# Hybrid decoder layer on one core: the second token tile's x/B/C, z and v behind the first tile's output projection, query weights by head, and an interleaved start of the expert gathers

## What is computed

```python
proj = x @ w_in                                  # 256 tokens x 1024
q, k, v, iq, ik, iw, z, xbc, dt = split(proj)
attn = dsa_attention(q, k, v, iq, ik, iw)        # 8 heads x 64, the 64 best causal keys per query by an indexer
ssd  = ssd_mixer(z, xbc, dt, ...)                # conv over 4 tokens, silu, scan in two chunks of 128, gated RMS norm
h    = layer_norm(alpha * x + concat(attn, ssd) @ w_out)
q2   = h @ wq                                    # PEER: 8 heads x 2 x 128
s1, s2 = q2[:, :, 0] @ k1.T, q2[:, :, 1] @ k2.T  # 128 keys a side
eidx, gate = best 16 of the 16 x 16 sums         # per token and head
out  = layer_norm(alpha * h + sum_k gelu(h . u[eidx_k]) * gate_k * v[eidx_k])
```

## Time and profile before

| | us |
|---|---|
| median of 3 runs | 832.15 (830.57 to 832.9) |
| the profiled execution | 831.91 |
| its span | 830.2 |
| busy in it: PE, DVE, ACT, POOL | 556.6, 555.6, 438.6, 275.5 |
| share of the chain that ended last: waits for gathered rows | 42% |

### The profile page before, as it was taken

The page is one execution under the profiler, slowest core; times in us unless marked ns, Lnnn a source line. Parts: engine busy times, 40 slices in busy tenths (PEclk is TensorE's granted clock), DMA queues, the critical chain, the costliest instruction groups (busy, mean ns, idle before and its releaser), DMA issues.

```text
span 830.2 us, 10063 instructions
## 1 busy us (share of the span) xinstructions
PE 556.6 (67%) x3215; PEld 465.0 (56%) x3215; DVE 555.6 (67%) x1387; ACT 438.6 (53%) x768; POOL 275.5 (33%) x267
## 2 busy tenths in 40 slices
PE   6999999999978546374745445525556555454596
PEld 3478565788978536364645444524455554454542
DVE  3499674675767585858495858469858576767454
ACT  1123560218657747565565657537756566565532
POOL 0000000125346444343525253514654435434400
PEclk9999999999999886776777686767776777767789
DMA  8994402198999999999999999999999999999992
GB/s 300 391 352 148 158 1 68 60 400 327 423 421 421 421 420 422 422 420 422 423 421 422 420 421 421 422 419 380 422 421 421 422 422 423 420 422 422 421 422 120
DMA packets 54276, 301.01 MB, mean 363 GB/s; under 512 B 5432, under 2 KB 7776, under 8 KB 21472
## 3 DMA queue, kind: packets, MB, share of 16 engines
q0 software_dynamic: 36864, 268.45, 78.2%
q1 hardware_dynamic: 16160, 31.92, 10.6%
q10 hardware_dynamic: 1216, 0.19, 0.1%
HBM read 299.49 MB, written 1.05 MB: 362 GB/s over the span
## 4 chain that ended last, share of the span: by engine, by line
DMA 43%; PE 32%; DVE 12%; issue 6%; ACT 4%; POOL 2%; DVEq 0%; SPq 0%; POOLq 0%; ACTq 0%
DMA arena<-in_expert_uv,expert 42%; PE bank L634 7%; PE bank L434 7%; PE bank L616 5%; DVE arena L1341 4%; PE bank L654 3%; PE bank L475 3%; PE bank L570 3%; POOL arena L401 2%; ACT arena L918 2%; ACT weight L908 1%; DMA arena<-in_w_idx 1%; PE bank L425 1%; PE bank L541 1%; PE bank L624 1%
## 5 line engine op out<-in xcount | busy, mean ns | idle before, releaser
L634 PE MATMUL bank<-ident,arena 128*128 128x128 f32 x1920 | 307.9, 334 | 248.6 <-ACT arena L918 248.4
L401 POOL DMA_INDIRECT arena<-in_expert_uv,expert x256 | 273.8, 1070 | 512.1 <-PE bank L634 271.1
L634 PEld LDWEIGHTS bank<-ident,arena 128*128 128x128 f32 x1920 | 288.5, 177 | 267.3 <-ACT arena L918 267.0
L1341 DVE SCALAR_TENSOR_TENSOR arena<-x_sb,arena 128x1024 f32<-128x1024 f32 x256 | 306.7, 1223 | 169.8 <-DMA arena<-in_expert_uv,expert 169.6
L918 ACT ACTIVATE arena<-arena,weight 128x1024 f32<-128x1024 f32 x240 | 256.2, 1138 | 1.9
L903 ACT ACTIVATE gelu<-dots 128x4 f32<-128x4 f32 (+2 forms) x68 | 13.9, 204 | 206.5 <-DVE arena L1341 205.9
L434 PE MATMUL bank<-arena,x_t 128*128 128x512 f32 (+1 forms) x160 | 66.6, 574 | 8.1 <-DMA arena<-in_w_idx 8.1
L616 PE MATMUL bank<-x_t,arena 128*128 128x128 f32 x512 | 58.8, 275 | 1.3 <-ACTq L878 1.3
L616 PEld LDWEIGHTS bank<-x_t,arena 128*128 128x128 f32 x512 | 57.9, 192 | 1.5 <-ACTq L878 1.5
L908 ACT ACTIVATE weight<-gelu,gate 128x1 f32<-128x1 f32 x256 | 55.1, 284 | 3.2
L434 PEld LDWEIGHTS bank<-arena,x_t 128*128 128x128 f32 x160 | 31.0, 197 | 40.1 <-issue 37.4
(11 more groups left out here) (195 smaller groups left out, 444.4 us busy)
## 6 DMA issues: line engine op xcount, KB each, us to landing
arena<-in_w_in SPq DMA_DIRECT2D x6, 2048.0 KB, 14.5
arena<-in_peer_wq SPq DMA_DIRECT2D x4, 2048.0 KB, 7.9
arena<-in_w_out SPq DMA_DIRECT2D x2, 2048.0 KB, 21.9
arena<-in_expert_uv,expert POOLq DMA_INDIRECT x256, 25.9
arena<-in_w_idx SPq DMA_DIRECT2D x2, 608.0 KB, 8.1
x_t<-in_x_columns SPq DMA_DIRECT2D x2, 512.0 KB, 6.6
x_sb<-in_x SPq DMA_DIRECT2D x1, 1024.0 KB, 17.3
ln_gb<-in_ln_g SPq DMA_DIRECT2D x2, 512.0 KB, 10.2
```

The lines of the kernel that those rows point to most:

```text
L401: pool.indirect_dma_start(out=arena[:, slot * SLOT:(slot + 1) * SLOT], out_offset=None, in_=expert_uv, in_offset=bass.IndirectOffsetOnAxis ...
L634: last = mm(banks[2 * tile + k // 4][:, (k % 4) * P:(k % 4 + 1) * P], lhsT=arena[:, at + k * P:at + (k + 1) * P], rhs=ident[:, :], is_tran ...
L1341: ins = stt(rows, x_rows[:, bass.ds(tile * D_MODEL, D_MODEL)], 1.0, rows, ALU.mult, ALU.mult, accum_out=dots[:, parity, j:j + 1])
```

## The change

- The first stage is split by tile. x/B/C, z and v of tile 1 (`project_xbc(1, n)`, `proj_z`, `proj_v`), its cb, y_off, y_diag and attention come behind tile 0's output product, layer norm, first queries and first scores. x/B/C is made as (tile, half of the channels), 32 products of 128 columns each; the last tap of the convolution and its bias move from DVE to ACT (`take_xbc`).
- Query weights come by head (`load_head`, 1 MB each) instead of by two heads. Head 0 lies in `mix`, heads 1 and 2 in slots 10 and 11, heads 3 to 7 one after the other in `mix`, each load behind tile 1's queries of the head before. Scores are made per head, those of heads 4 to 7 within units 2 to 4.
- The first gathers go into slots 12 to 15, 4 and 5 (`first_slots`), each used up to three times in units 0 and 1. Units 0 and 1 work in groups of two slots, interleaved by hand with the rest of tile 1 on PE, ACT and DVE. The units from 2 to 8 are unrolled; before, units 3 to 6 were a loop.
- q's weights are loaded into the buffers of x and of the norm's rows, the input and index weights in four parts instead of two. All copies of probabilities are on ACT.

```diff
-    jobs += [("proj_k", 0)] + idx_dots[0] + [("proj_k", 1)] + idx_dots[1]
-    jobs += [("T_qk", 0, 0), ("T_qk", 0, 1), ("proj_xbc", 0), ("consts",), ("proj_xbc", 1)]
...
+    jobs = [("proj_idx", t) for t in both] + [("proj_q", t) for t in both] + [("T_idx", t) for t in both] + [("consts",)]
+    jobs += [("proj_k", 0)] + idx_dots[0] + [("proj_k", 1)] + idx_dots[1] + sums[0]
+    jobs += [("T_qk", 0, 0), ("T_qk", 1, 0), ("proj_xbc", 0, 0)] + logits[0] + [("T_qk", 0, 1), ("T_qk", 1, 1), ("proj_xbc", 0, 1)]
...
+    jobs += [("proj_xbc", 1, 0), ("T_h", 0, 0), ("T_h", 0, 1), ("peer_q", 0, 0), ("key_scores", 0, 0)] + sums[1]
+    jobs += [("proj_xbc", 1, 1), ("proj_z", 1), ("proj_v", 1), ("cb", 1), ("T_xs", 1), ("y_off",), ("y_diag", 1)]
...
-    first = list(range(12))
-    return 3 * first + list(range(12, SLOTS)) + list(range(8))
+    front = [12, 13, 14, 15, 4, 5]
+    return front + front + [0, 1, 2, 3] + front + [6, 7, 8, 9, 0, 1, 2, 3, 10, 11]
...
+        def head_weights(h):
+            if h in (1, 2):
+                return view(arena, (9 + h) * SLOT, KT, 2 * P)
+            return view(mix, 1024, KT, 2 * P)
...
+            def load_head(h):
+                sp.dma_start(head_weights(h), wq_rows[:, :, 2 * P * h:2 * P * (h + 1)]).then_inc(w_in_sem[f"wq{h}"], 16)
...
+            for part in range(4):
+                ks = slice(2 * part, 2 * part + 2)
+                sp.dma_start(x_t[:, ks, :], x_columns.rearrange("(k p) n -> p k n", p=P)[:, ks, :]).then_inc(idx_in[part], 16)
+                sp.dma_start(chunk(places["idx"], IDX_COLS + SSD_HEADS)[:, ks, :],
+                             w_idx.rearrange("(k p) n -> p k n", p=P)[:, ks, :]).then_inc(idx_in[part], 16)
...
+            wait_job(sp, ("idx_dot", 1, 3))
+            sp.wait_ge(rel_used, TILES)
+            load_head(0)
+            wait_job(sp, ("proj_xbc", 1, 0))
+            load_head(1)
+            load_head(2)
+            for h in range(3, PEER_HEADS):
+                wait_job(sp, ("peer_q", 1, 0 if h == 3 else h - 1))
+                load_head(h)
...
-            last_readers = {0: ("T_y", 1), 2: ("pv", 1), 4: ("out", 1, 0), 6: ("out", 1, 1), 8: ("peer_q", 1, 0),
-                            10: ("peer_q", 1, 1), 12: ("peer_q", 1, 2), 14: ("peer_q", 1, 3)}
...
+            last_readers = {0: ("T_p", 1, 3), 1: ("pv", 1), 2: ("T_y", 1), 3: ("T_y", 1), 4: ("proj_v", 1), 5: ("proj_v", 1),
+                            6: ("out", 1, 1), 7: ("out", 1, 1), 8: ("out", 1, 0), 9: ("out", 1, 0), 10: ("peer_q", 1, 1),
+                            11: ("peer_q", 1, 2), 12: ("proj_xbc", 1, 1), 13: ("proj_xbc", 1, 1), 14: ("proj_z", 1), 15: ("proj_z", 1)}
...
+            project_xbc(1, 0, range(0, 2))
+            transposed_h(0, 0)
+            project_xbc(1, 0, range(2, 3))
+            transposed_h(0, 1)
+            queries(0, 0)
+            scores_of_keys(0, 0)
+            project_xbc(1, 0, range(3, 4))
+            running_sums(1)
+            project_xbc(1, 1)
+            project(("proj_z", 1), "z", 1)
+            project(("proj_v", 1), "v", 1, ks=range(0, 4))
+            pe.wait_ge(silu_ready, 4)
+            cb_and_xs(1)
...
+            sum_group(0, 0)
+            transposed_probs(1)
+            sum_group(0, 1)
+            queries(0, 1)
             attend(1)
-            scores_of_keys(("first_scores",), 0, 0, range(2))
+            scores_of_keys(0, 1)
+            sum_group(0, 2)
             transposed_y(1)
             transposed_attention(1)
-            queries(("peer_q", 0, 0), 0, 0, range(2, 4))
             for half in range(2):
-                project_out(1, half)
-            scores_of_keys(("key_scores", 0, 0), 0, 0, range(2, 4))
-            queries(("peer_q", 0, 1), 0, 1)
-            transposed_h(1)
-            pe.wait_ge(h_t_ready, 2 * TILES)
...
             root_of_variance(0)
+            take_h(0)
+            take_queries(0, 0)
+            take_scores(0, 0)
+            exp_logits(1)
+            wait_job(act, ("out", 0, 1))
+            take_xbc(1, 0)
+            exp_gate(act, 0)
+            take_xbc(1, 1)
+            exp_decay(1)
+            silu_xbc(1, 0)
+            silu_z(1)
+            silu_xbc(1, 1)
+            weigh_slots(0, 0, 0)
             take_v(1)
-            take_h(0)
+            weigh_slots(0, 0, 1)
...
+            decay_argument(1)
+            convolve(1, 0)
+            convolve(1, 1)
+            dot_slots(0, 0, 0, 0)
+            source_side(1)
+            dot_slots(0, 0, 0, 1)
+            dot_slots(0, 0, 0, 2)
+            take_ssd(1)
+            take_attention(1)
+            dot_slots(0, 0, 0, 3)
+            scores_in(0, 1)
+            route_sides(1)
+            dot_slots(0, 0, 0, 4)
+            route_pairs(1)
+            finish_gate(1, 1)
+            dot_slots(0, 0, 0, 5)
+            half_stats(1, 0, add_mixed)
+            dot_slots(0, 0, 0, 6)
+            half_stats(1, 1, add_mixed)
+            normalise(1, 1, h_ready)
             dve.wait_ge(h_ready, 2 * TILES)
             dve.sem_inc(ln1_done, 1)
-            groups = slot_groups(False)
-            dot_slots(0, 0, 0, groups[0])
```

More of the change, by code:

```diff
@@ L64, in psum_jobs @@
-    jobs += [("proj_v", 0), ("y_diag", 0), ("state",), ("pv", 0)] + [("T_p", 1, n) for n in range(4)]
-    jobs += [("T_y", 0), ("T_attn", 0)] + sums[1] + [("cb", 1), ("T_xs", 1)] + [("out", 0, half) for half in range(2)]
-    jobs += [("proj_v", 1)] + [("T_h", 0, half) for half in range(2)] + [("y_off",), ("y_diag", 1), ("first_q",)]
-    jobs += [("pv", 1), ("first_scores",), ("T_y", 1), ("T_attn", 1), ("peer_q", 0, 0)]
-    jobs += [("out", 1, half) for half in range(2)] + [("key_scores", 0, 0), ("peer_q", 0, 1)] + [("T_h", 1, half) for half in range(2)]
@@ new lines, in project_out, with transposed_h, queries @@
+                for k in ks:
+                    last = mm(bank(job)[:, :], lhsT=mix_t[t][:, k, :], rhs=weight_rows(f"out{half}", k),
+                              start=k == 0, stop=k == KT - 1)
+                if ks[-1] == KT - 1:
+                    last.then_inc(full(job), 1)
+            def transposed_h(t, half):
+                pe.wait_ge(h_ready, 2 * t + half + 1)
+                transposes(("T_h", t, half), [x_sb[:, t, k * P:(k + 1) * P] for k in range(4 * half, 4 * half + 4)])
+            def queries(t, h):
+                job = ("peer_q", t, h)
+                pe.wait_ge(w_in_sem[f"wq{h}"], 16)
+                pe.wait_ge(h_t_ready, 2 * (t + 1))
+                wait_bank(pe, job)
+                for n in range(2):
@@ new lines, in _ @@
+            project(("proj_z", 0), "z", 0, ks=range(0, 5))
+            y_diagonal(0)
+            job = ("state",)
+            pe.wait_ge(b_nat_ready, 1)
+            wait_bank(pe, job)
+            for g in range(GROUPS):
+                heads = slice(g * GROUP_HEADS, (g + 1) * GROUP_HEADS)
+                last = mm(bank(job)[:, g * 256:(g + 1) * 256], lhsT=b_nat[:, g, :],
+                          rhs=xdt_end[:, heads, :].rearrange("p a b -> p (a b)"), start=True, stop=True)
+            last.then_inc(full(job), 1)
@@ new lines, in tap, with take_xbc @@
+            def tap(k, c):
+                return conv_t[:, k * CT + c:k * CT + c + 1]
+            def take_xbc(t, n):
+                job, now = ("proj_xbc", t, n), slice(t * P, (t + 1) * P)
+                wait_job(act, job)
+                run(xbc_raw[:, 4 * n:4 * n + 4, CONV_WIDTH - 1 + t * P:CONV_WIDTH - 1 + (t + 1) * P], bank_view(job, 4, P), ACT.Copy)
+                for c in range(4):
+                    last = run(xbc[:, 4 * n + c, now], bank(job)[:, c * P:(c + 1) * P], ACT.Identity,
+                               scale=tap(CONV_WIDTH - 1, 4 * n + c), bias=tap(CONV_WIDTH, 4 * n + c))
+                last.then_inc(free(job), 1)
@@ L799, in take_v, with silu_z @@
+            def silu_z(t):
+                job = ("proj_z", t)
+                wait_job(act, job)
+                run(z_silu[:, t, :], bank(job)[:, :], ACT.Silu).then_inc(free(job), 1)
+                act.wait_ge(free(job), use(job))
+                act.sem_inc(z_ready, 1)
             def take_v(t):
@@ L1370, in _ @@
                 before = count[0]
[L1371 removed]
+                dot_unit(u, u // PEER_HEADS, u % 2)
                 per_unit = count[0] - before
[L1374 to L1381 removed]
@@ L1394 @@
+            for half in range(2):
+                half_stats(TILES - 1, half, add_sum)
+            normalise(TILES - 1, 2 * TILES - 1, result_ready)
 def kernel(**inputs):
```

829 lines of the change are left out of this document (415 added, 414 removed).

## The result

| | before | changed kernel |
|---|---|---|
| median of the runs, us | 832.52 (830.57 to 834.65, 4 runs) | 869.76 (869.13 to 872.67, 4 runs) |
| ratio, 95% interval | | 1.0445 (1.0423 to 1.0468) |
| profiled execution: span, time | 830.2, 831.9 | 867.9, 869.6 |
| first gather, eleventh gather | 162.4, 194.9 | 152.6, 192.7 |

The change costs 37 us. The forecast was 835.6 with a range to 843: the sign was right, the size was off by 34 us.

What follows compares the result with a forecast made beforehand. DMA traffic of expert rows at 421 GB/s was taken to bound the kernel after the ramp, PE before it. 831.9 - 11.3 (ramp) + 12.5 (late head loads) + 2.5 (ln2) = 835.6 us, range 822 to 843.

Steps and rivals of the forecast that it cites:

- What bounds: After the ramp: end equals time the DMA queue fills plus remaining bytes at 421 GB/s; before that PE bounds.
- The walk to the first gather: Block-by-block durations from the start: first scores at 129.7 us, routing to 139.5, first gather at 144.2.
- (a): Before the second index product: PE waits 7.5 us for VectorE to free the constants' bank, plus 1.7 us slow clock.
- (b): Tile 0's attention output: T_attn(0) is taken by ScalarE behind the root of squares, a wait of 3.0 us.
- (c): After first scores: xbc(1,1) waits 3.7 us for xbc(1,0)'s bank, emptied by ScalarE behind exp_logits(1).
- Clock falls at (b) and (c): PE's clock might slow behind these two waits, 0 to 1.7 us each; taken as 0.
- First to eleventh gather: The new ramp, slots freed by tile 1's projections: first gather at 144.2 us, eleventh at 183.9.
- the gain of 11.3 us: Ramp up to 200 us: 15.7 gathers done, 4.5 more than before, so 11.3 us less.
- Late head loads, +12.5: Query weights of heads 3 to 7 load after tile 1's queries, five times 1.05 MB at 421 GB/s: 12.5 us more.
- ln2, +2.5: Two ln2 rows load behind tile 1's norm near 210 us, not in the 164 to 200 stretch: 2.5 us more.
- Late heads' products in units 2 to 4: They cost PE 7.2 us in a unit of 40 where it is half idle, hidden by 16 slots: 0.
- Starved behind the ramp: Rival, chance 0.15: unit 1's routing over 3 us late stops the DMA, 839 to 845; decided by gather 17 after 201.

Runs made afterwards that it cites:

- e8: Changed kernel with the edits of e1, e2, e5_consts and e6, loading only one of eight k steps of query weights of heads 3 to 7: 820.77 us.
- e5_consts: Changed kernel with VectorE emptying the constants' bank ahead of tile 0's selection, not behind the rope of k1: 864.60 us.
- e6: Changed kernel; ScalarE takes T_attn(0) before root of squares, x/B/C (1,0) before exp_logits(1); VectorE empties y_off, y_diag banks before dots of slots 4, 5: 852.55 us.
- e4: Changed kernel with only one of eight k steps of the query weights of heads 3 to 7 loaded: 867.36 us.
- e14: Changed kernel with PE's query products of heads 3 to 7 cut to one of eight k steps, all loads kept: 858.79 us.
- e2: Changed kernel with ScalarE scaling a group's slots before taking the queries beside it, in units 1 to 4: 854.15 us.
- e1: Changed kernel with ScalarE's exponential for the gate of unit 2 ahead of the scores of (1, 0), not behind (1, 2): 868.37 us.
- e10: Changed kernel with edits of e1, e2, e5_consts, e6, products of heads 5 to 7 one per unit, more ramp scaling and sums moved ahead: 825.13 us.

## Why the prediction was wrong

*What bounds*: right as far as it went. With the queue full the end is a sum over bytes, which e8 bears out (9.0 us, good to some 3, for 10.9 us of bytes). I took for granted that it stays full behind the ramp.

*The walk to the first gather* (144.2, measured 152.6): **8.4 us short**. The waits were right or nearly so: (a) 7.5 predicted, 6.2 measured; (b) 3.0, 3.2; (c) 3.7, 4.0. At (a) two errors cancel, by luck: the wait is 1.3 shorter, and the slow clock behind it costs about 3 us (the same instructions in e5_consts) and not 1.7. The step of the walk that failed is under Bounds: "Clock falls at (b) and (c)", of which "I take 0". Both came: the attention half of the output product took 8.73 us behind (b), 7.11 in e6, and x/B/C (1,1) 9.86 behind (c), 7.41 in e6. That is 1.6 + 2.5 = 4.1 us. The reason I gave, that these waits are "shorter than the one idle time that shows a fall", misread the trace of before. It is not the only one. My reading of PE's timeline behind the ramp ended at 262 us, and just behind that stands

```profile
264.60 5.16 PE L634 MATMUL bank<-ident,arena 128*128 128x128 f32 x32 [3.08 <-ACT arena L918]
```

with the clock at 0.50 from 265 to 267, and another behind 3.33 us at 273.09. Another 1.4 of the walk is the input: PE ended its first projections at 32.54 (the start of the transposes that follow), 0.3 later than before, not 1.1 earlier. Up to 1 us of that is the chance of one execution. The last 2 to 3 are small hand-overs that I did not count one by one, and no run assigns them.

*First to eleventh gather*: 39.7 us predicted, 40.1 measured. The wait for y_off's bank, 5.8 with a clock fall behind it, was 7.05. So gather 11 came 8.8 us late, and the gain of 11.3 us was all but gone: 8.8 / 2.49 = 3.5 of the 4.5 gathers.

*Late head loads, +12.5*: the price of a full queue, and in this kernel partly hidden (e4: 3.5 of 10.9). *ln2, +2.5*: issued at 375.4, not near 210, since SP's queue holds them behind the last head load; the bytes are the same.

*The steps that failed most* are two that I put at nothing. One is the ramp: my walk ends with the 17th gather and takes the queue as full from there, and 12.8 us are lost from 240 to 300. The other is "Late heads' products in units 2 to 4 cost PE 7.2 us in a unit of 40 (16 x 2.49) where it is half idle, and 16 slots hide them: 0"; 11.6 us are lost from 300 to 400, and e14 brings 9.5 of these back. I compared PE's busy share with its room and did not walk ScalarE's order beside PE's behind 200, although both lists were in front of me. There take_queries stands ahead of weigh_slots in every group that has queries, so that two engines take turns though neither is near full. PE is busy 111.5 of the 160 us from 240 to 400 there, ScalarE 90.5, and neither share tells it. (The Trainium skill, "Perfetto Trace Analysis", section Optimization Strategy, says that the same gap repeating on the engine that should be saturated can mean too few buffers. PE's waits do repeat here, every 10.3 us, and the DMA stands still again and again, near 252, 272, 310 and 362 us, but e2 closes most of these gaps with the same sixteen slots.) 24.3 us is what the two cost; e2 gives back 16.1 of them by turning ScalarE's order, e14 12.1 by shortening the products. The sum with the late ramp and these is 835.6 + 8.8 + 24.3 = 868.7, against 869.6 in the profiled execution. A count of bytes agrees: up to 240 us the changed kernel has moved 224 GB/s x 240 us against 248 x 240, 5.8 MB or 13.7 us less, and 13.7 + 24.3 = 38.0, where the spans differ by 37.7.

*The rivals*: "Starved behind the ramp" had the sign and the ScalarE order in it, but its mechanism, a late routing of unit 1, is not what happened: gather 17 did go out late, at 207.0, past its deciding point of 201, but it stood 14.3 us behind the eleventh, against 15 in my walk, and the rate from 200 to 240 was 419. The queue starved 40 us later and for another reason. Two of the signs that I had named as proving me wrong came: gather 11 left after 190, and the rate dipped between 200 and 300.

What stays open: some 7 of the 24.3 us that neither e1 nor e2 gives back. In e2's trace they lie mostly from 240 to 260 (3.1 us) and from 300 to 320 (2.1). e10 closes them, but with the ramp and the late groups edited too, so no run assigns them.
